# Attention: the rotary part of the query folded by a product, its rounded and low part stacked in one stationary tile, five score products in place of six

## The reference, cut to what matters

```python
MLA_HEADS, MLA_NOPE, MLA_ROPE, MLA_V = 8, 128, 64, 128

def rope_tail(t, cos, sin):
    nope, pe = jnp.split(t, [MLA_NOPE], axis=-1)
    p1, p2 = jnp.split(pe.astype(F32), 2, axis=-1)
    cs, sn = cos[:, None, :], sin[:, None, :]
    pe = jnp.concatenate([p1 * cs - p2 * sn, p2 * cs + p1 * sn], axis=-1)
    return jnp.concatenate([nope, pe], axis=-1)

def block_attention(q, k, v):
    scale = dq ** -0.5
    def one(qi):                       # one block of 128 queries
        s = jnp.einsum('bhqd,bhkd->bhqk', qi, k).astype(F32) * scale
        p = jax.nn.softmax(s, axis=-1)
        return jnp.einsum('bhqk,bhkd->bhqd', p.astype(v.dtype), v)

# in mla_mixer: q, k normalised per head by rmsnorm, then the rotary tail; yl = attention @ w_out
```

## Time and profile before

| | before |
|---|---|
| median of 3 runs | 3482.76 us (3482.6 to 3483.79) |
| the profiled execution | 3483.15 us, its span 3481.4 us |
| TensorE busy | 3162.9 us, 91% of the span |
| VectorE, ScalarE, GpSimd busy | 66%, 28%, 35% |
| mean granted clock of TensorE | 0.962 |
| heads of the attention, from the first turned tile to the last values | about 2072 to 2648 us of the span |

### The profile page before, as it was taken

How to read it: one execution, slowest core, us unless ns; L and a number is a source line. 1 busy time by engine, 2 the same in 40 slices (tenths; PEclk the granted TensorE clock), 3 DMA queues, 4 the chain that set the end, 5 groups by cost and what they waited for, 6 DMA issues and landing times. The chain is left out here.

```text
span 3481.4 us, 54123 instructions
## 1 busy us (share of the span) xinstructions
PE 3162.9 (91%) x19758; PEld 2620.6 (75%) x19758; DVE 2290.7 (66%) x3205; ACT 968.7 (28%) x1517; POOL 1228.5 (35%) x1023
## 2 busy tenths in 40 slices
PE   5989988896889999999997779999998799999998
PEld 3879966665778888888886548877887577877876
DVE  7976067886366666666666346666664587777777
ACT  4111245544141111111111434444442221111111
POOL 1322145551232222222220132212121376777664
PEclk8999999998999999999999879999999899999999
DMA  4558220004111111111100200000002011111111
GB/s 193 195 179 292 70 78 2 2 2 159 34 40 43 42 36 36 37 41 36 36 30 12 74 9 5 6 6 5 6 13 79 32 43 54 54 54 48 48 48 73
DMA packets 64269, 196.37 MB, mean 56 GB/s; under 512 B 7680, under 2 KB 20864, under 8 KB 62848
## 3 DMA queue, kind: packets, MB, share of 16 engines
q1 hardware_dynamic: 47280, 163.83, 14.2%
q10 hardware_dynamic: 16848, 30.56, 2.6%
HBM read 175.49 MB, written 18.87 MB: 56 GB/s over the span
## 5 line engine op out<-in xcount | busy, mean ns | idle before, releaser
L1414 DVE SCALAR_TENSOR_TENSOR resid<-ps,mod,resid 128x256 f32<-128x256 f32 x528 | 342.0, 661 | 259.4 <-PE ps L1310 259.2
L1317 PE MATMUL ps<-hf_hi,up_hi 128*128 128x512 f32 (+1 forms) x1056 | 376.8, 357 | 16.4 <-DVE hf_lo L288 11.7
L1317 PE MATMUL ps<-hf_lo,up_hi 128*128 128x512 f32 (+1 forms) x1056 | 376.5, 357 | 0.0
L1317 PE MATMUL ps<-hf_hi,up_lo 128*128 128x512 f32 (+1 forms) x1056 | 375.1, 355 | 0.0
L1775 DVE SCALAR_TENSOR_TENSOR resid<-ps,mod,resid 128x512 f32<-128x512 f32 x352 | 255.8, 749 | 95.7 <-PE ps L1583 95.0
L1604 PE MATMUL ps<-x_hi,w_spare 128*128 128x512 f32 x824 | 289.0, 394 | 12.9 <-DVE x_lo L1700 10.9
L1285 POOL TENSOR_SCALAR up_hi<-up_raw 128x1024 fp32r<-128x1024 f32 x44 | 47.5, 1080 | 684.4 <-PE ps L1317 650.3
L820 POOL TENSOR_TENSOR k_decayed<-decay,qk 128x256 f32<-128x256 f32 (+1 forms) x240 | 194.1, 838 | 192.6 <-ACT decay L985 192.6
L131 DVE CUSTOM_DVE_ANT_0 ps<-adaw_ring,cond,adab 128x1024 f32<-128x1024 f32 x128 | 205.8, 1608 | 57.3 <-DMA adaw_ring<-in_adaw 46.9
L1317 PEld LDWEIGHTS ps<-hf_hi,up_hi 128*128 128x128 f32 x1056 | 201.6, 191 | 42.9 <-issue 17.6
L1317 PEld LDWEIGHTS ps<-hf_hi,up_lo 128*128 128x128 f32 x1056 | 200.8, 190 | 28.5
(11 more groups left out here) (313 smaller groups left out, 8721.8 us busy)
## 6 DMA issues: line engine op xcount, KB each, us to landing
up_raw<-in_up SPq DMA_DIRECT2D x88, 512.0 KB, 3.5
adaw_ring<-in_adaw SPq DMA_DIRECT2D x80, 512.0 KB, 4.2
dn_raw<-in_dn SPq DMA_DIRECT2D x44, 512.0 KB, 3.5
vr<-vr_out ACTq DMA_DIRECT2D x80, 128.0 KB, 2.4
adaw_first<-in_adaw SPq DMA_DIRECT2D x16, 512.0 KB, 21.9
wvr_raw<-in_wvr SPq DMA_DIRECT2D x8, 1024.0 KB, 7.3
x<-in_xT ACTq DMA_DIRECT2D x8, 640.0 KB, 16.7
r<-vr ACTq DMA_DIRECT2D x10, 512.0 KB, 3.8
```

The lines of the kernel that those rows point to most:

```text
L1317: mm = pe.matmul(c.psf[:, at:at + w], a[:, half, k, :], b[:, k, t:t + w], start=(k == 0 and a is up_hi and b is h_hi), stop=(k == KD - 1 a ...
L1414: dve.scalar_tensor_tensor(resid[:, m, t:t + w], c.ps[:, 6 + j % 2, 0:w], c.mod[:, gate + m, cond[t]:cond[t] + 1], resid[:, m, t:t + w], A ...
```

## The change

A new piece `q_fold` multiplies `q_turn` by the fold matrix, a plain float32 product of 512 columns; its result has the 64 rotary query features on the upper 64 partitions and again on the lower 64. ScalarE rounds it into `q_hi` part 1, and VectorE then replaces the lower 64 partitions there by the low part. So `q_hi` part 1 holds rounded part and low part, stacked, and one pass with `k_hi` part 1 gives both of their products. The fifth and last pass of a group is that of the upper 64 partitions of `q_hi` part 1 with the upper 64 of `k_lo` part 1. GpSimd's rounding, `q_pe_low` and the rotary half of `q_lo` go. The fold matrix comes with one more transfer, issued by SyncE after the latents are done. In the order of the pieces `q_sum` 0 moves from unit 20 to 17, `q_pe` 1 from 21 to 20, `q_fold` stands at 15 and 21, `q_sum` 1 stays at 23.

```diff
-           13: (("k_norm", 2),), 14: (("q_pe", 0),), 15: (("k_low", 1),), 16: (("k_low", 0), ("q_pe_low", 0)),
-           18: (("q", 1),), 20: (("q_sum", 0),), 21: (("q_pe", 1),), 22: (("q_pe_low", 1),), 23: (("q_sum", 1),)}
+           13: (("k_norm", 2),), 14: (("q_pe", 0),), 15: (("q_fold", 0), ("k_low", 1)), 16: (("k_low", 0),),
+           17: (("q_sum", 0),), 18: (("q", 1),), 20: (("q_pe", 1),), 21: (("q_fold", 1),), 23: (("q_sum", 1),)}
 PIECES = (("k", 0), ("k", 1), ("k", 2), ("k_sum", 0), ("k_sum", 1), ("k_sum", 2), ("q", 0), ("q_pe", 0),
-          ("q", 1), ("q_sum", 0), ("q_pe", 1), ("q_sum", 1), ("v", 0), ("v", 1), ("v", 2))
+          ("q_fold", 0), ("q_sum", 0), ("q", 1), ("q_pe", 1), ("q_fold", 1), ("q_sum", 1), ("v", 0), ("v", 1), ("v", 2))
...
         load(0, 0)
+        sp.wait_ge(*latents_set)
+        sp.dma_start(fold[:, :], a["eye"][3]).then_inc(fold_in, 16)
         heads(sp, body)
...
             elif step == "q_pe":
-                pool.wait_ge(dve_read, h * NV + READS["q_pe", part])
-                pool.nop(nofuse=True)
-                pool.tensor_scalar(q_hi[:, 1, part * BANK:(part + 1) * BANK], q_turn[:, :], 1.0, 1.0,
-                                   ALU.mult, ALU.mult).then_inc(q_pe_hi_set, 1)
                 pool.wait_ge(q_sq_set, h * 4 + SQUARES["q_pe", part])
...
+            elif step == "q_fold":
+                if begins(h) and part == 0:
+                    pe.wait_ge(fold_in, 16)
+                mm = pe.matmul(work, fold[:, :], q_turn[:, :], start=True, stop=True)
...
                 if t % 4 == 0:
-                    pe.wait_ge(q_lo_set, h * 2 + (t // 4 + 1))
+                    pe.wait_ge(dve_read, h * NV + READS["q_fold", t // 4])
...
-            n = 0
-            for part in range(2):
-                for qq, kk in split_passes(q_hi, q_lo, k_hi, k_lo):
-                    mm = pe.matmul(c.psf[:, at:at + w], qq[:, part, t * P:(t + 1) * P],
-                                   kk[:, slot, part, k0:k0 + w], start=(n == 0), stop=(n == 5))
-                    n += 1
+            tile, keys = slice(t * P, (t + 1) * P), slice(k0, k0 + w)
+            passes = ((q_hi[:, 0, tile], k_hi[:, slot, 0, keys]), (q_hi[:, 0, tile], k_lo[:, slot, 0, keys]),
+                      (q_lo[:, tile], k_hi[:, slot, 0, keys]), (q_hi[:, 1, tile], k_hi[:, slot, 1, keys]),
+                      (q_hi[0:ROPE, 1, tile], k_lo[0:ROPE, slot, 1, keys]))
+            for n, (qq, kk) in enumerate(passes):
+                mm = pe.matmul(c.psf[:, at:at + w], qq, kk, start=(n == 0), stop=(n == len(passes) - 1))
...
+            elif step == "q_fold":
+                act.activation(q_hi[:, 1, half], work, ACT.Copy).then_inc(q_pe_hi_set, 1)
...
-            elif step == "q_pe_low":
+            elif step == "q_fold":
                 dve.wait_ge(q_pe_hi_set, h * 2 + (part + 1))
-                dve.tensor_tensor(q_lo[:, 1, half], q_turn[:, :], q_hi[:, 1, half].bitcast(F32),
-                                  ALU.subtract).then_inc(q_lo_set, 1)
+                dve.tensor_tensor(q_hi[ROPE:P, 1, half], work[ROPE:P, :], q_hi[ROPE:P, 1, half].bitcast(F32),
+                                  ALU.subtract).then_inc(dve_read, 1)
```

More of the change, by code:

```diff
@@ L2042, in attention @@
     q_hi = c.at("q_hi", 53, [P, 2, SEQ], F32R)
-    q_lo = c.at("q_lo", 61, [P, 2, SEQ], F32R)
+    q_lo = c.at("q_lo", 61, [P, SEQ], F32R)
+    fold = c.at("fold", 65, [P, P])
     k_hi = c.at("k_hi", 69, [P, 2, 2, T], F32R)
@@ L2068, in attention @@
     (wv_in, wk_in, wq_in, w_hi_set, w_split, consts_set, piece_done, act_read, dve_read, k_sq_set, k_logged,
-     k_rstd_set, k_normed, kp_set, k_hi_set, k_lo_set, q_sq_set, q_added, q_hi_set, q_pe_hi_set, q_lo_set,
+     k_rstd_set, k_normed, kp_set, k_hi_set, k_lo_set, q_sq_set, q_added, q_hi_set, q_pe_hi_set, fold_in,
      q_rstd_set, v_hi_set) = c.sems(
@@ L2072, in attention @@
         "k_logged", "k_rstd_set", "k_normed", "kp_set", "k_hi_set", "k_lo_set", "q_sq_set",
-        "q_added", "q_hi_set", "q_pe_hi_set", "q_lo_set", "q_rstd_set", "v_hi_set")
+        "q_added", "q_hi_set", "q_pe_hi_set", "fold_in", "q_rstd_set", "v_hi_set")
     (s_done, max_set, neg_set, p_set, inv_set, normed, turned, pth_set, ptl_set, pv_done, o_set) = c.sems(
@@ L2439, in prepare @@
                 dve.wait_ge(q_hi_set, h * 2 + (part + 1))
-                dve.tensor_tensor(q_lo[:, 0, half], work, q_hi[:, 0, half].bitcast(F32), ALU.subtract
+                dve.tensor_tensor(q_lo[:, half], work, q_hi[:, 0, half].bitcast(F32), ALU.subtract
                                   ).then_inc(dve_read, 1)
@@ L2443, in prepare @@
                 dve.wait_ge(q_sq_set, h * 4 + SQUARES["q_pe", part])
-                if part or not begins(h):
-                    dve.wait_ge(q_lo_set, h * 2 + part)
                 dve.scalar_tensor_tensor(q_turn[:, :], work, norms[:, 1:2],
```

## The result

The changed kernel takes 3485.34 us, the median of 20 runs (3482.94 to 3493.26); the kernel before, run beside it, 3483.31 (20 runs, 3480.22 to 3488.48). The ratio is 1.0013, interval [1.0007, 1.0019]: 2 us slower, inside the 0.2% that I called no change, inside the range, and 11 us above the forecast of 3474. The runs of after fall into two clusters, 13 between 3482.9 and 3486.6 and 7 between 3490.4 and 3493.3.

What follows compares the result with a forecast made beforehand. TensorE's order of work sets the time, apart from waits and the low clock behind them. Per head -1.55 us, seven times -10.9, with +1 before the first and +1 in the last: -9, to 3474 us; range 3448 to 3488.

Steps and rivals of the forecast that it cites:

- Once: Before the first head, uncovered folds, copies and subtractions less the waits for GpSimd: +1 us, between -1 and +3.
- Heads: Seven heads of the second layer's attention, each 1.55 us shorter: -10.9 us together.
- Tile 5: In each head `k_low` 1 starts 2.2 us later behind the fold's low part; the tile gets 1.5 us longer.
- tiles 0 to 3: Score passes in each head's first four tiles: +0.14, +0.32, +0.25 and +0.25 us, with the 64-partition excursion at 0.30.
- tile 6: No slack in each head: +0.65 less 0.1 us for `q_pe` 1 replacing `q_sum` 0, +0.32 for score passes.
- tile 4: In each head VectorE's `pt_lo` ends this tile, not the scores: 0 change.
- the price of the pass over 64 partitions: In each score group, going to 64 partitions and back costs 0.30 us; a tile gets 0.32 longer, not 0.58 shorter.
- the first rival: The 64-partition pass costs what other passes do: -4.3 us a head, -32 in all, 3451 us; chance 0.28.
- the stall in tile 7 and its clock: The wait for GpSimd's squares at `q_sum` 1 and the low clock behind it go: -4.9 us a head, tile 10.7.
- The second rival: The clock still falls in tile 7, costing 20 us over seven heads: +11, 3493 us; chance 0.12.
- The third: The `q_sum` 1 wait only moves to VectorE's low part; if 0.7 us later, +5 over seven heads; no separate chance.
- what I took as the mean of before: Mean head 74.10 us, 1.19 above the one examined; the excess put into tile 7 as longer low-clock stretches.

Runs made afterwards that it cites:

- e12: The kernel before with 160 do-nothing instructions, which were merged into one, in TensorE's wait before the first head; 3483.83 us.
- e16: The kernel before with 297 waits on a value long reached before the first piece, moving its loop by 148 places; 3502.92 us.
- e1: The changed kernel with the last pass of a score group over all 128 partitions; 3457.95 us, ratio to before 0.9926.
- e13: The changed kernel with 193 waits on a value long reached before the first head, moving its loop by 96 places; 3504.86 us.
- e7: The kernel before with filler passes, results unread, behind each piece of the first head's preparation; 3478.54 us, ratio to before 0.9984.
- e2: The kernel before with the moves of the pieces alone, six passes and no fold; 3454.04 us, ratio to before 0.9917.
- e3: The changed kernel with the last pass over all 128 partitions and `k_low` 1 ahead of the fold's low part in unit 15; 3450.32 us, ratio 0.9901.
- e17: e8 with 80 more filler passes of 128 columns before the first piece, its loop 256 places later than in after; 3457.23 us.
- e18: e6 with 80 more filler passes of 128 columns before the first piece, its loop 256 places later than in after; 3492.86 us.
- e6: The changed kernel with filler passes, results unread, behind each piece of the first head's preparation; 3481.48 us, ratio to before 0.9992.
- e8: e3 with filler passes, results unread, behind each piece of the first head's preparation; 3448.65 us, ratio to before 0.9903.

## Why the prediction was wrong

**The step that failed first is "Once": "+1, between -1 and +3" for the pieces before the first head.** It was +9.1 in the profiled execution, 8.1 of the 16.3 us by which the rows of the table miss the forecast. Three things were wrong in it. The chain of pieces, two folds, copies and subtractions less the waits for GpSimd, costs 3.35 us at the low clock (e12 and e16 against after), not 1. The score passes of tiles 0 and 1, which stand in this stretch too, got no term; they took 4.3 us more, because the low clock went on through them. And before had the full clock for part of the chain, worth 1.5 us, which nothing in the new order secures. "More at the low clock" stood in the text and never entered the sum. It went on into the first head: the clock rose at 2088, tile 0 took 8.7 us in place of 6.6, and its period 74.93 in place of 72.9 to 73.2.

The median lies 5.3 us under the profiled execution, and all profiles of this kernel are of the upper cluster. If those 5.3 us lie in this stretch, which is argued and not shown, "Once" is some 3 us off at the median and the heads, 6.5 us off, are the larger miss. Why the clock rose early in some executions and late in others stays open.

**Heads: -4.4 in place of -10.9.** 1.9 of the gap is that first head. The rest is small errors of one sign in each head: the mean of before was 518.28 / 7 = 74.04, that of the six later heads of after 73.16, so -0.9 where I said -1.55. Tile 5 cost +1.85, not +1.5 (VectorE idles for the copy longer than I had it); tile 7 is 10.9, not 10.7; tiles 0 to 3 +1.1, not +0.96; tile 6 +0.9 as said; tile 4 nothing as said.

**Right: the price of the pass over 64 partitions.** 0.28 us by the trace, 0.30 by the sum, and e1 confirms it from the other side. With that the first rival (a free pass, chance 0.28, 3451) fell. The Trainium skill's page TensorEngine Tiling (Array Packing), section Tiling Modes, says that a change of mode drains the engine. The trace agrees: the weights of the 64 partitions and those behind them are not loaded beside a pass (2159.47 and 2159.89). The Trainium skill's page TensorE: Matmul & The Clock Gate, section LDWEIGHTS (loading the stationary operand), has the time of a load depend on its columns and not on its rows. The trace agrees with that as well, 0.18 us for 64 rows and 0.19 for 128. What failed is what I drew from it, that the excursion would then cost nothing: the load takes as long as any other but is not hidden.

**Right: the stall in tile 7 and its clock.** -4.7 where -4.9 was said, the clock at 1.00 in the heads from 2088 us on, no wait at `q_sum`. That tile 7 hardly depends on the price of the pass, as the first rival had it (-5.0), e1 shows. The second rival (the clock still falls) did not come up in the heads; a low clock did decide much of the result, but before them. The third, a wait that moves to VectorE's low part, is not in the waits of after, but it lies just beneath them: with the excursions gone (e1) it is there, 0.46 us.

**Right in part for another reason: what I took as the mean of before.** I put the 1.19 us by which the mean period exceeded my head down to longer stretches of low clock behind the stall. Two of the periods (76.35 and 75.28) hold the hole at the turn of the loop, and are 3.4 and 2.4 us above 72.9; only the 1.5 us of a third (74.4) fit my reading. The hole vanished in after because its loop lies where its code is kept. Put elsewhere (e13), the seven heads take 519.3 us, 1.0 *more* than before, although the first is 2.0 shorter there. Before's own heads take 514.4 to 518.4 us by the profile (e16, e12, e7, before). So the gain of 4.4 us in the heads would be a loss without this, and the forecast's sum has that luck in it.

**What the change is worth part by part.** The moves alone bring 31 us (e2). The fold and the fifth pass take it all back: with all 128 partitions in that pass 27 us return (e1), and with `k_low` 1 first the kernel is 35 us under before (e3). Even so nothing here shows that the fold and the five passes are worth anything beside the moves. e3 is 3.7 us under e2, the intervals overlap, and e2's profile has two holes that lengthen its heads by 5.4 and 3.9 us where e3's has none. Without a hole the period is 68.0 in e2 and 69.0 in e3: five passes save 0.1 to 0.4 us in tiles 0 to 3 and 6, but tile 7, 9.07 us in e2, is 10.8 with the fold, and tile 5 is 10.3 in place of 9.8. No run has e2 with the filler passes or with its loop in another place, so which of the two is faster with both mended stays open.

## What to carry to other kernels

Do not shorten the contraction of one pass between full ones: here 64 partitions in place of 128 cost 0.28 us each time and more than the saved pass gave. Run the parts of a change by themselves: here a reordering that came along with it was worth 31 us alone, and nothing shows the rest of the change to be worth anything beside it. When TensorE has stretches in which it mostly waits, count them at both levels of the clock, with all the work that stands in them, and take their part of the range from the difference. Compare two orders of work only where rows show them at the same level. And if engines loop over long code, look at the packets of the instruction queue within the loop and for idle time with no releaser where it jumps back, before a gain or loss of a few us is ascribed to the work that was changed.

## What the runs showed of the hardware that I had not expected

- The instruction queue moved 1.33 MB in 81 packets in after, 16 KB each. With the loop in one place, nothing is fetched from its second round to its end; 96 instructions later, 18 packets come between 2290 and 2590 us and TensorE stands 2.26 and 1.99 us at the turns; 256 later (e17, e18) it is kept again. The Trainium skill's page Runtime: NRT & Kernel Launch, section Instruction fetch mechanics, has blocks of 16 KiB, and a stall where a taken branch leads out of a window of two such pages. The trace agrees on the blocks and on the stall. The window of two pages it does not bear out: one round of the loop in after has 1601 records of matmuls and weight loads (2304.37 to 2450.67 us), more than six blocks of 256, and nothing is fetched for it again. Where exactly the limit lies was not found; before, whose loop is longer, was fetched again at each of the places tried.
- In the heads, where TensorE is otherwise busy, behind each hole of 1.9 to 2.7 us with nothing in it the clock was at 0.50, whatever the hole's cause: the earlier trace rows for a wait, e2, e6, e8 and e13 for the hole at the turn. It stayed there for some 3 us in e6 and e13 and for over 6 in e2 (2279 to 2285 us). Hole and low clock together cost 3.4 to 5.4 us a time.
- Two executions with the same work of TensorE in the 29.87 us up to a point had different clocks at that point (2043.62 in before, 2045.26 in after). What decides it was not found.
- A wait on a value long reached is not free: 193 of them in a row, merged into 96 instructions, added 10 us on TensorE, 0.1 us for each instruction left.
